# Two 64-wide heads on the two halves of TensorE's array, and a recurrence cut into pieces between the steps of an attention

## The reference, cut to what matters

```python
def step(state, inp):
    r_t, w_t, k_t, v_t, a_t, b_t = inp
    sa = jnp.einsum("bhvk,bhk->bhv", state, a_t)
    state = state * w_t[:, :, None, :] + sa[..., None] * b_t[:, :, None, :] + v_t[..., None] * k_t[:, :, None, :]
    return state, jnp.einsum("bhvk,bhk->bhv", state, r_t)
```

## Time and profile before

| | us |
|---|---|
| median of 3 runs (3025.43 to 3028.09) | 3027.68 |
| profiled execution | 3027.91 |
| its span, first to last instruction | 3026.1 |
| TensorE busy | 2659.0 |
| VectorE busy | 1861.2 |
| ScalarE busy | 1412.3 |
| mean granted TensorE clock | 0.905 of 2.4 GHz |

### The profile page before, as it was taken

One profiled execution on the slowest core, in us unless ns is written; L12 is line 12 of the kernel. 1 busy time (PEld: TensorE's weight loads), 2 busy tenths in 40 slices (PEclk: granted clock), 3 DMA queues, 4 the chain that ended last, 5 costly groups with the idle time before them and its releaser, 6 DMA issues. The chain is left out here.

```text
span 3026.1 us, 37637 instructions
## 1 busy us (share of the span) xinstructions
PE 2659.0 (88%) x14146; PEld 2222.7 (73%) x14146; DVE 1861.2 (62%) x2377; ACT 1412.3 (47%) x1835; POOL 363.6 (12%) x241
## 2 busy tenths in 40 slices
PE   7788886998889789878898978659999999999998
PEld 6447664897887479755797957647888888888886
DVE  3653334554757444443453754457898898988987
ACT  3231112443554144312443431127777777777776
POOL 3101120001444000000000422220000000000000
PEclk9877778998999899986999978769999999999999
DMA  6600011554423055330554510038999999999996
GB/s 226 207 28 1 1 42 51 193 174 141 140 94 116 15 174 187 133 121 0 186 176 144 182 51 1 1 154 325 368 384 365 372 380 372 372 376 370 382 368 226
DMA packets 180226, 574.54 MB, mean 190 GB/s; under 512 B 10975, under 2 KB 80735, under 8 KB 136989
## 3 DMA queue, kind: packets, MB, share of 16 engines
q1 hardware_dynamic: 175884, 558.01, 50.0%
q0 software_dynamic: 3264, 11.80, 1.5%
q10 hardware_dynamic: 976, 3.33, 0.3%
HBM read 564.98 MB, written 6.29 MB: 189 GB/s over the span
## 5 line engine op out<-in xcount | busy, mean ns | idle before, releaser
L2851 DVE TENSOR_TENSOR moe_weights_low<-ring,moe_weights_high 128x1024 fp32r<-128x1024 f32 x672 | 782.4, 1218 | 109.4 <-ACT moe_weights_high L2806 107.0
L2806 ACT CAST moe_weights_high<-ring 128x1024 fp32r<-128x1024 f32 x672 | 685.8, 1051 | 106.1 <-PE banks L254 102.5
L252 PE MATMUL banks<-moe_weights_high,moe_rows_high 128*128 128x512 f32 x896 | 354.5, 396 | 2.5 <-DVE moe_rows_low L2836 2.5
L254 PE MATMUL banks<-moe_weights_low,moe_rows_high 128*128 128x512 f32 x896 | 350.1, 391 | 0.0
L253 PE MATMUL banks<-moe_weights_high,moe_rows_low 128*128 128x512 f32 x896 | 349.5, 390 | 0.0
L252 PE MATMUL banks<-ffn_x_high,ffn_weights_high 128*128 128x256 f32 x1056 | 300.1, 284 | 15.4 <-DVE ring_low L2405 15.4
L253 PE MATMUL banks<-ffn_x_high,ring_low 128*128 128x256 f32 x1056 | 299.6, 284 | 0.0
L254 PE MATMUL banks<-ffn_x_low,ffn_weights_high 128*128 128x256 f32 x1056 | 299.2, 283 | 0.0
L2405 DVE TENSOR_TENSOR ring_low<-ring,ffn_weights_high 128x2048 fp32r<-128x2048 f32 x66 | 148.0, 2288 | 137.6 <-ACT ffn_weights_high L2377 137.6
L252 PEld LDWEIGHTS banks<-ffn_x_high,ffn_weights_high 128*128 128x128 f32 x1056 | 202.6, 192 | 18.8 <-issue 16.4
L253 PEld LDWEIGHTS banks<-ffn_x_high,ring_low 128*128 128x128 f32 x1056 | 202.0, 191 | 2.3
(11 more groups left out here) (523 smaller groups left out, 5152.2 us busy)
## 6 DMA issues: line engine op xcount, KB each, us to landing
ring<-in_moe_gate_pieces SPq DMA_DIRECT2D x112, 1024.0 KB, 7.2
ring<-in_moe_up_pieces SPq DMA_DIRECT2D x112, 1024.0 KB, 7.4
ring<-in_moe_down_pieces SPq DMA_DIRECT2D x112, 1024.0 KB, 7.2
ring<-in_ffn_w SPq DMA_DIRECT2D x66, 1024.0 KB, 7.8
ring<-in_od_w_in SPq DMA_DIRECT2D x10, 2048.0 KB, 8.3
ring<-in_o_w_in SPq DMA_DIRECT2D x8, 2048.0 KB, 8.6
ring<-in_e_ffn_w_gate SPq DMA_DIRECT2D x11, 1024.0 KB, 5.5
ring<-in_e_ffn_w_up SPq DMA_DIRECT2D x11, 1024.0 KB, 8.1
```

The lines of the kernel that those rows point to most:

```text
L252: pe.matmul(out_, lh, rh, start=start, stop=False)
L254: return pe.matmul(out_, lh, rl, start=False, stop=stop)
L2806: act.copy(hi[:, b * 1024:(b + 1) * 1024], piece).then_inc(sems["hi_done"], 1)
L2851: dve.tensor_tensor(lo[:, b], piece, hi[:, b].bitcast(F32), ALU.subtract).then_inc(sems["lo_done"], 1)
```

## The change

- **Decay mixer.** Heads 2i and 2i+1 form a pair, with their transposed slices on partitions 0 to 63 and 64 to 127 of one 128 x 512 tile (`tv`). `turn_pair` transposes 128-column slices of both at once and copies them once; `pair_scores` multiplies both heads, head by head in alternation, each from its own partitions into its own bank. Pair i+1 is transposed ahead of pair i's scores. The two groups for the inversion are now the even and the odd heads; the strict products alternate between them and end together. State, `carry`, and the copy of y follow the new layout.
- **Third mixer.** `paired_attention` replaces `attention` here. GpSimd writes each key head twice side by side, so that one transpose puts it on both halves of the partitions; keys are transposed once for all heads, queries in pairs; scores of two heads alternate between the halves. The transposes of the weights leave out the block above the diagonal. In each of its first five steps one piece of the recurrence is appended (`during`): `decay_rates`, `one_less`, `square_root`, `inputs`, `gated_scan`. The reciprocal is issued as four quarters, two in each of the second and third pieces, and the scans as two and two.

The diff, cut to what the prediction speaks of:

```diff
+        def paired_attention(qkv, H, KVH, N, scale, y, ready, mask, sink, during):
+            HK = H + KVH
+            heads = [{n: room(TT) for n in ("m", "nm", "sum", "es")} for _ in range(H)]
+            bufs = [{n: room(512) for n in ("s", "p", "pt")} for _ in range(4)]
+            qT, kT = [room(T) for _ in range(2)], room3(KVH, T)
+            twice = room(TT * KVH * P).rearrange("p (t j n) -> p t j n", t=TT, j=KVH)
+            half = [slice(g * N, g * N + N) for g in range(2)]
+            copied, weights, inverse, turned_p = {}, {}, {}, {}
+            q_used, p_used, pt_used = {}, {}, {}
...
+                for due in unseen(pool, ready):
+                    pool.wait_ge(*due)
+                for t in range(TT):
+                    pool.tensor_copy(twice[:, t].rearrange("p j (s n) -> p j s n", s=2),
+                                     qkv[:, t, H * N:HK * N].rearrange("p (j n) -> p j n", n=N).unsqueeze(2).to_broadcast([P, KVH, 2, N])
+                                     ).then_inc(*G.tick())
+            doubled = G.at()
...
+            def turn_keys():
+                bank = take_bank()
...
+                    for j in range(KVH):
+                        for t in range(TT):
+                            last = pe.transpose(bank.ap[:, j * T + t * P:j * T + (t + 1) * P], twice[:, t, j, :], ident)
+                    last.then_inc(*M.tick())
...
+                    act.wait_ge(*turned)
+                    act.copy(kT, bank.ap[:, 0:KVH * T].rearrange("p (j t) -> p j t", t=T)).then_inc(*S.tick())
...
+            def turn_queries(p):
+                bank = take_bank()
...
+                    for t in range(TT):
+                        last = pe.transpose(bank.ap[:, t * P:(t + 1) * P], qkv[:, t, p * P:(p + 1) * P], ident)
+                    last.then_inc(*M.tick())
...
+                    for due in unseen(act, q_used.get(p - 2)):
+                        act.wait_ge(*due)
+                    act.wait_ge(*turned)
+                    act.copy(qT[p % 2], bank.ap[:, 0:T]).then_inc(*S.tick())
...
+            def scores(p):
+                two = [take_bank() for g in range(2)]
+                @block.tensor
+                def _(pe):
+                    for due in unseen(pe, two[0].free, two[1].free, copied[p]):
+                        pe.wait_ge(*due)
+                    for t in range(TT):
+                        for g in range(2):
+                            last = pe.matmul(two[g].ap[:, t * T:(t + 1) * T], qT[p % 2][half[g], t * P:(t + 1) * P],
+                                             kT[half[g], 2 * p * KVH // H, :], start=True, stop=True)
+                            if t == TT - 1:
+                                last.then_inc(*M.tick())
+                have = q_used[p] = M.at()
+                for g in range(2):
+                    weigh(2 * p + g, two[g], have)
...
+            def weigh(i, bank, have):
+                b, sm = bufs[i % 4], heads[i]
...
+                    for due in unseen(act, have, p_used.get(i - 4)):
+                        act.wait_ge(*due)
+                    for t in range(TT):
+                        act.activation(b["p"][:, t * T:(t + 1) * T], sv[:, t, :], ACT.Exp, bias=sm["nm"][:, t:t + 1],
+                                       accum_out=sm["sum"][:, t:t + 1]).then_inc(*S.tick())
+                    act.activation(sm["es"], sm["nm"], ACT.Exp, bias=sink[:, i:i + 1]).then_inc(*S.tick())
+                weights[i] = S.at()
...
+            def turn_weights(i):
+                b, sm = bufs[i % 4], heads[i]
+                bank = take_bank()
...
+                    dve.tensor_tensor(sm["sum"], sm["sum"], sm["es"], ALU.add).then_inc(*V.tick())
+                    dve.wait_ge(*V.at())
+                    dve.reciprocal(sm["sum"], sm["sum"]).then_inc(*V.tick())
...
+                    for kt in range(TT):
+                        for t in range(kt, TT):
+                            at = kt * T + t * P
+                            last = pe.transpose(bank.ap[:, at:at + P], b["p"][:, t * T + kt * P:t * T + (kt + 1) * P],
+                                                ident)
...
+                    act.copy(b["pt"][:, 0:T], bank.ap[:, 0:T]).then_inc(*S.tick())
+                    act.copy(b["pt"][:, T + P:2 * T], bank.ap[:, T + P:2 * T]).then_inc(*S.tick())
...
+            turn_keys()
+            pairs = H // 2
+            for n in range(pairs + 3):
+                if n < pairs:
+                    turn_queries(n)
+                if 0 <= n - 1 < pairs:
+                    scores(n - 1)
+                for back, step in ((2, turn_weights), (3, values)):
+                    if 0 <= n - back < pairs:
+                        for g in range(2):
+                            step(2 * (n - back) + g)
+                if n < len(during):
+                    during[n]()
+            return V.at()
...
+                for i in range(H // 2):
+                    c = slice(i * P, (i + 1) * P)
+                    pe.matmul(bank.ap[:, i:i + 1], decay[:, 0, c], const("halves")[:, 1:2], start=True, stop=False)
+                    last = pe.matmul(bank.ap[:, i:i + 1], decay[:, 1, c], const("halves")[:, 0:1], start=False, stop=True)
...
+            tv = room3(H // 2, 512)
             idle = [None, None]
+            half = [slice(g * N, g * N + N) for g in range(2)]
+            head = lambda g, j: slice((2 * j + g) * N, (2 * j + g + 1) * N)
+            by_side = y.rearrange("p t (j s n) -> p t s j n", s=2, n=N)
...
+                groups = [dict(work[g], mv=work[g]["TTm"].rearrange("p (h n) -> p h n", h=4)) for g in range(2)]
+                copied = []
+                def turn_pair(i):
+                    c = slice(i * P, (i + 1) * P)
+                    bank = take_bank()
+                    @block.tensor
+                    def _(pe):
+                        for due in unseen(pe, bank.free, scaled):
+                            pe.wait_ge(*due)
+                        for m, x in enumerate((lr, k, kk, r)):
+                            last = pe.transpose(bank.ap[:, m * P:(m + 1) * P], x[:, t, c], ident)
+                        last.then_inc(*M.tick())
+                    turned = M.at()
+                    @block.scalar
+                    def _(act):
+                        for due in unseen(act, turned, idle[0], idle[1], scaled):
+                            act.wait_ge(*due)
+                        act.copy(tv[:, i, :], bank.ap).then_inc(*S.tick())
+                    bank.free = S.at()
+                    copied.append(S.at())
...
+                def pair_scores(i):
+                    one = [tv[half[g], i, :] for g in range(2)]
+                    two = [take_bank() for g in range(2)]
+                    @block.tensor
+                    def _(pe):
+                        for due in unseen(pe, two[0].free, two[1].free, copied[i]):
+                            pe.wait_ge(*due)
+                        for g in range(2):
+                            pe.matmul(two[g].ap[:, 0:256], one[g][:, 0:P], one[g][:, 256:512], start=True, stop=True)
+                        for g in range(2):
+                            pe.matmul(two[g].ap[:, 256:512], one[g][:, P:256], one[g][:, 256:512], start=True,
...
+                            dve.tensor_tensor(groups[g]["mv"][:, i, :], two[g].ap, const("quad"), ALU.mult).then_inc(*V.tick())
+                        two[g].free = groups[g]["masked"] = V.at()
...
+                turn_pair(0)
+                for i in range(H // 2):
+                    if i + 1 < H // 2:
+                        turn_pair(i + 1)
+                    pair_scores(i)
+                two = [take_bank() for g in range(2)]
+                @block.tensor
+                def _(pe):
+                    for due in unseen(pe, two[0].free, two[1].free):
+                        pe.wait_ge(*due)
+                    for j in range(4):
+                        for g in range(2):
+                            last = pe.matmul(two[g].ap[:, j * P:(j + 1) * P], tv[half[g], j, 256:384], tv[half[g], j, 0:P],
                                              start=True, stop=True)
-                        last.then_inc(*M.tick())
+                            if j == 3:
+                                last.then_inc(*M.tick())
+                for g, w in enumerate(groups):
+                    w["NT"], w["N"] = w["mv"][:, :, 0:P], two[g]
...
+                    old = lambda j: state[half[g], j * N:(j + 1) * N]
...
-                            c = slice((4 * g + j) * N, (4 * g + j + 1) * N)
-                            last = pe.matmul(bank.ap[:, j * N:(j + 1) * N], mv[:, j, 256:384], v[:, t, c],
+                            last = pe.matmul(bank.ap[:, j * N:(j + 1) * N], mv[:, j, 256:384], v[:, t, head(g, j)],
                                              start=True, stop=(t == 0))
                             if t:
```

(64 more changed lines are left out.)

206 lines of the change are left out of this document (97 added, 109 removed).

## The result

The changed kernel takes 2954.85 us (median of 4 runs, 2953.76 to 2956.54), the kernel before 3027.06 us beside it: ratio 0.976, 95% interval 0.975 to 0.978, 72.2 us faster. The forecast was 2971.2 with a range down to 2959, so the change was worth 16 us more than forecast. The profiled execution has a span of 2952.1 us.

A forecast was written before the change was run, and what follows sets the result against it. It took low-clock TensorE work, idle during ScalarE's copies, to bound the decay mixer, and recurrence then attention in a line the third. 3027.9 - 36.5 - 20.6 + 0.4 = 2971.2 us; range 2959 to 2990.

The forecast's parts named there:

- the second step: Stages after the two changed ones: they follow in data order with no transfer inside, so shift whole, with no further gain.
- I take overlap, and half way between its two clocks: 36.5.: Decay mixer: halves overlap, saving 31.2 us at the low clock or 41.9 at the high; 36.5 taken.
- my own walk at the high clock: Decay mixer, overlap with high clock: first half ends at 222.7, second takes 10.9 us; 41.9 us saved.
- the walk for the halves in turn: Decay mixer's second half of the tokens, no overlap, low clock: 22.1 us against 32.2, 10.1 saved.
- eight records take five slots: Decay mixer's scores: if a record waits only for its own half, a pair takes 2.13 us in place of 3.41.
- the strict products I leave at full cost: Decay mixer's 16 strict-product records: no overlap gain, 3.41 us, since their weight loads are as long as the products.
- The rule of the Trainium skill: Decay mixer: array tiles run weight loads and matmuls in parallel, so a pair takes four slots, 3.4 us less in all.
- walked at 20.6: Third mixer: attention between the recurrence's pieces, output's transposes begin at 1391.0 and not 1411.55, 20.6 us saved.
- Halves in turn: Rival: the two halves never overlap, saving 20.9 us in the decay mixer and 19.7 in the third; 2987.7 us, chance 0.26.
- The keys' doubling: Third mixer: GpSimd's two new key copies beside VectorE's convolution cost 0 to 0.8 us; 0.4 taken.
- draining: Rival, both mixers: each of 64 changes of half drains the array, 0.27 us each; around 3005 us, chance 0.05.
- stalls: Rival, third mixer: a late square-root piece makes VectorE wait at the scores, half the gain lost; 2981 us, chance 0.09.

The follow-up runs named there:

- The run on one half: Changed kernel, but in the decay mixer scores and strict products of a pair's second head read the first head's half of the partitions: 2978.75 us, ratio 0.984.
- the one on one half: Changed kernel, but in the third mixer's attention the scores of a pair's second head read the first head's half: 2962.44 us, ratio 0.979.
- the one in turn: Changed kernel, but the recurrence's five pieces are issued all ahead of the banded attention, heads still paired: 2964.04 us, ratio 0.980.
- the two with products ahead: Changed kernel with decay-mixer products not needing the inverse moved ahead of the inversion: 2924.13 us; the same with the output's products left behind it: 2927.4 us.

## Why the prediction was wrong

The direction, the two mechanisms and the order of their sizes were right; the sum was 16 us short, and two of its steps failed. With the measured 43.0 and 21.9 us in it the sum would have been 2963.0, inside the range. What carried the time out of it are the 8 us that the second step put at nothing.

**"I take overlap, and half way between its two clocks: 36.5."** The parts gave 21.2 + 21.8 = 43.0. Of the 6.5 missing, 5.4 is the clock: my own walk at the high clock gave 41.9, the first half ending at 222.7 (it ended at 221.69 after a start at 213.36, 8.3 us for 8.9, below the 9 that I had named as the least) and the second in 10.9 (10.4, with the low spell at its start that I had taken). I had set the two clocks against each other as equals, though in the earlier trace rows every long stretch with dense work and a low clock was one with 64 rows at a time (the 4.8 us from 247.40, dense and low as well, are the inversion's start, before its clock rose). The run on one half shows that putting the heads on both halves decides the clock here: 22.1 us at 0.50, which is to the tenth the walk for the halves in turn. The other 1.1 cannot be assigned: in the seven profiles with the same instructions there the two parts together took 17.8 to 20.4 us (18.8 in this one), so they saved 41.4 to 44.0. Two counts in the walk were wrong all the same: "eight records take five slots" (four) and "the strict products I leave at full cost" (half). The rule of the Trainium skill, TensorEngine Tiling (Array Packing), section Key Properties, that I weighed and did not take would have given the four, and the trace agrees with 0.86 us a pair at the high clock. It was worth less than its 3.4 us, which were counted at the low clock, and VectorE's masks end last.

**"All later stages follow these two in data order ..., so they shift whole."** They are shorter by some 8 us: 2.4 and 3.2 behind the third mixer, 2.6 behind the decay mixer. The first two are shown to belong to the third mixer's edits (with them 389.7 to 389.8 and 293.5 to 293.8 in every run with the whole of them, without them 414.0 and 296.9), and to hang on how the stage itself runs: on one half 296.6, in turn 297.1. From the recurrence to the end the changed kernel saved 27.4 us by its span for a stage 21.9 shorter, the one on one half 20.9 for 20.3, the one in turn 17.2 for 16.4, so the extra comes with the whole change alone. Over the delta-rule mixer the granted clock's mean goes from 0.76 to 0.77: its low spells add up to 136.5 us in place of 143.3. As an estimate, work through 6.8 us at half the rate costs 3.4 us, about the 3.2 saved. Which trait of the stage sets the later low spells is open, its length against them included. The 2.6 is near the scatter of that stretch (381.5 to 383.7 in the runs with the decay mixer's edits, the shifts taken off, and 383.8 to 384.0 in the two with products ahead, against 384.3 to 384.6 in the three runs that lack the edits or their overlap), so how much of it belongs to the change is not settled. The 1.4 ahead of both is scatter.

**The third mixer** was walked at 20.6 and gave 21.9; "39 to 40 us" was 38.3, "VectorE busy over 85%" 87%, the square root lay 20.0 us behind the first step (20.5 in the walk). Halves in turn was walked at 0.9 more, measured 1.6. What I had not seen is why it pays: I had written the walk as one of interleaving, and three quarters come from the attention in pairs. The keys' doubling, taken at 0.4, cost nothing that shows: the stretch up to the recurrence's first step is as long as before.

**Two slips of its own.** The lower end of the forecast's own range, 2960, is 2962.4 by the terms named beside it (41.9 and 24). And the clock did fall inside the inversions, a sign that I had named as wrong: for 6.8 us near the start of each (from 223.0 and 294.6). Before, it was low there too, for the inversions' first 9.2 and 7.9 us, so the sign told nothing.

**The rivals.** Halves in turn is excluded by 0.86 us for eight records, where half of 3.41, one after another at the high clock, would be 1.7; draining by the same rows, since scores follow each other without a gap over changes of half; stalls by the stage of 38.3 us.

## What to carry to other kernels

Where a stage's products use half of the array's rows, put two independent ones on the halves: in the decay mixer it was worth a factor of four, two in slots and two in the granted clock. Count the gain in the clock as a case of its own, with the rows of before at either clock beside it; half of it was a poor guess here. It does not come everywhere: in the third mixer, where TensorE waited for VectorE, the stage stayed at 0.55. When TensorE waits ahead of a serial stage, look behind that stage for products that don't need it; moved ahead they fill the wait and leave a short end (20 and 26 us became 4.4 and 4.3). An engine that is busy 87% of a stage need not end it: issue one of its instructions twice and see whether the stage grows, which tests the place where that instruction stands. And time the unchanged stages too: here they gave 8 of 74 us.

## What the runs showed of the hardware that I had not expected

- The two halves take records by themselves: with four records of the other half ahead of it in the program a product started 0.013 us behind the first of them, and with eight ahead it started with the fifth. Alternating the halves in the program gains 0.5 us on 16 records and nothing that shows in the kernel's time.
- Fp32 weight loads of the two halves lie beside each other too: 16 records of 64x128 by 128 columns in 1.06 us, 0.066 each.
- TensorE busy 21.97 of 22.00 us, its 64-row products one at a time, was granted 0.50 throughout; with two at a time it was granted 1.00 while busy 87%.
- The low spells behind the third mixer lie at the same distance from the recurrence's first step, to within 0.1 us, in the nine profiles with the whole third mixer, whether that step comes at 1274.8 or at 1349.5 us, and change when the stage in between runs otherwise.
